# Additions moved to VectorE, unadded squares on TensorE, earlier weight splits, DMA-made tables and a later wait at the stage borders of a two-block transformer kernel

## What is computed

```python
def rms_norm(x, g):
    xf = x.astype(jnp.float32)
    y = xf * lax.rsqrt(jnp.mean(xf * xf, axis=-1, keepdims=True) + RMS_EPS)
    return (y * g.astype(jnp.float32)).astype(x.dtype)
...
        x = x + rms_norm(m, mix_post_g[layer])
        f = conv_glu_ffn(rms_norm(x, ffn_pre_g[layer]), ffn_w_in[layer], ffn_conv_w[layer],
                         ffn_conv_b[layer], ffn_w_out[layer])
        x = x + rms_norm(f, ffn_post_g[layer])
```

## Time and profile before

| | us |
|---|---|
| median of 3 runs (lowest to highest) | 1732.46 (1731.77 to 1732.62) |
| profiled execution, its own time | 1733.53 |
| its span in the trace | 1731.8 |
| PE busy | 1641.2 (95%) |
| DVE, ACT, POOL busy | 1028.8 (59%), 701.7 (41%), 286.4 (17%) |
| chain that ended last, on PE | 87% |

### The profile page before, as it was taken

The page is one execution under the profiler, slowest core; times in us unless marked ns, Lnnn a source line. Parts: engine busy times, 40 slices in busy tenths (PEclk is TensorE's granted clock), DMA queues, the critical chain, the costliest instruction groups (busy, mean ns, idle before and its releaser), DMA issues.

```text
span 1731.8 us, 21441 instructions
## 1 busy us (share of the span) xinstructions
PE 1641.2 (95%) x8098; PEld 1321.4 (76%) x8098; DVE 1028.8 (59%) x1860; ACT 701.7 (41%) x1370; POOL 286.4 (17%) x233
## 2 busy tenths in 40 slices
PE   6899999999898898999999998999998999999996
PEld 6678888888676686888888886866665788888875
DVE  4766666543768666666663266576666455554364
ACT  3444444332346644444442243243344243333252
POOL 2411111000402213111110025000001021110021
PEclk8899999999899999999999999999999999999998
DMA  4133333333121123333332324221110223333321
GB/s 142 37 97 96 96 97 97 104 97 92 52 70 34 38 61 86 97 98 97 97 96 95 96 63 110 67 55 38 43 39 24 86 82 96 97 97 98 98 91 61
DMA packets 89343, 139.28 MB, mean 80 GB/s; under 512 B 8596, under 2 KB 28564, under 8 KB 89240
## 3 DMA queue, kind: packets, MB, share of 16 engines
q1 hardware_dynamic: 86464, 133.56, 25.9%
q10 hardware_dynamic: 2776, 4.35, 0.9%
HBM read 135.78 MB, written 2.10 MB: 80 GB/s over the span
## 4 chain that ended last, share of the span: by engine, by line
PE 87%; DVE 6%; POOL 2%; issue 2%; ACT 1%; DMA 0%; SPq 0%; ACTq 0%; POOLq 0%; DVEq 0%
PE ps L399 23%; PE ps L401 22%; PE ps L400 22%; PE ps L1809 2%; PE ps L1811 2%; PE ps L1810 2%; POOL M L529 1%; PE ps L1492 1%; PE ps L1515 1%; PE ps L419 1%; PE ps L1535 1%; DVE Hl L514 1%; PE ps L412 1%; DVE M L681 1%; PE ps L456 1%
## 5 line engine op out<-in xcount | busy, mean ns | idle before, releaser
L387 DVE TENSOR_TENSOR wl<-raw,wh 128x512 fp32r<-128x512 f32 (+1 forms) x466 | 361.6, 779 | 481.0 <-ACT wh L376 480.9
L376 ACT ACTIVATE wh<-raw 128x512 fp32r<-128x512 f32 (+1 forms) x466 | 292.1, 628 | 648.6 <-PE ps L401 639.4
L399 PE MATMUL ps<-Hh,wh 128*128 128x512 f32 x1276 | 508.8, 399 | 17.6 <-DVE Hl L514 9.3
L400 PE MATMUL ps<-Hl,wh 128*128 128x512 f32 x1276 | 501.5, 393 | 0.0
L401 PE MATMUL ps<-Hh,wl 128*128 128x512 f32 x1276 | 501.3, 393 | 0.0
L399 PEld LDWEIGHTS ps<-Hh,wh 128*128 128x128 f32 x1276 | 242.6, 190 | 80.3 <-DVE Hl L514 14.9
L401 PEld LDWEIGHTS ps<-Hh,wl 128*128 128x128 f32 x1276 | 242.2, 190 | 52.0 <-issue 0.2
L400 PEld LDWEIGHTS ps<-Hl,wh 128*128 128x128 f32 x1276 | 242.6, 190 | 50.0 <-issue 0.9
L399 PE MATMUL ps<-AH,wh 128*128 128x512 f32 x456 | 177.6, 389 | 0.0
L401 PE MATMUL ps<-AH,wl 128*128 128x512 f32 x456 | 177.4, 389 | 0.0
L400 PE MATMUL ps<-AL,wh 128*128 128x512 f32 x456 | 177.4, 389 | 0.0
(11 more groups left out here) (291 smaller groups left out, 1925.3 us busy)
## 6 DMA issues: line engine op xcount, KB each, us to landing
raw<-in_w_in SPq DMA_DIRECT2D x216, 256.0 KB, 2.7
raw<-in_w_out SPq DMA_DIRECT2D x104, 256.0 KB, 2.6
raw<-in_w_up SPq DMA_DIRECT2D x64, 256.0 KB, 2.6
raw<-in_w_down SPq DMA_DIRECT2D x32, 256.0 KB, 2.7
raw<-in_w_q SPq DMA_DIRECT2D x16, 256.0 KB, 2.6
raw<-in_w_o SPq DMA_DIRECT2D x16, 256.0 KB, 2.6
raw<-in_w_pg SPq DMA_DIRECT2D x16, 256.0 KB, 2.8
X<-in_xT SPq DMA_DIRECT2D x8, 256.0 KB, 6.2
```

Source lines behind the costliest of these rows:

```text
L376: e.activation(split_in[n][0][:, 0:width], raws[n % NRAW][:, 0:width], ACT.Copy, scale=1.0 if gain is None else gain).then_inc(s_hi, 1)
L387: e.tensor_tensor(wl[:, 0:width], raw, wh[:, 0:width].bitcast(F32), ALU.subtract).then_inc(s_lo, 1)
L399: e.matmul(b, wh[:, o:o + w], xh, start=k == 0, stop=False, skip_group_check=joined)
L400: e.matmul(b, wh[:, o:o + w], xl, start=False, stop=False, skip_group_check=joined)
```

## The change

- `X_ON_POOL` is empty for the three borders with halves: all their additions of M to x are on DVE, and the order in `dve_new_rhs` is scale, low part of the column before, add.
- `rhs_sums` adds nothing there: PE takes the eight squares unadded, four calls of `mean_square` after piece 4 and four after piece 6.
- In the closing, DVE adds the squares of tiles 4 to 6 into `T[5]` (`add_square`), and PE sums `T[5]` and tile 7 alone, for each half; `first_four` is gone.
- Seven more pairs of buffers in each of the three borders instead of three. A table `due` lists what is split at each piece: from 14 pieces before `kv` and `z` and from 8 before `in1`, two pieces are split at a time, so that all eight pieces of the new group are split before the closing, and none is due at its pieces 0 to 4.
- `STAT_BANK` is the last bank instead of the last but one, and the wait for `RB` stands before the last of the four tiles of the next piece (`late`).
- The scaled tables come by DMA: `dist` grows from 256 KB to 2 MB, `cmp` from 62 to 496 KB. The DMA issues of ACT at the kv and z borders move from ahead of the border to piece 4 of the group.

The core of the diff:

```diff
--- before.py
+++ after.py
-for _n, _w in (("ident", 128), ("dist", 512), ("swa", 128), ("turn", 128), ("cmp", 124), ("sel", 512), ("band", 1088)):
+for _n, _w in (("ident", 128), ("dist", 4096), ("swa", 128), ("turn", 128), ("cmp", 992), ("sel", 512), ("band", 1088)):
...
-        more = [(sub(f"xh{i}", [P, NPIECE], 24576 + 4096 * i, F32R), sub(f"xl{i}", [P, NPIECE], 26624 + 4096 * i, F32R))
-                for i in range(3)]
+        more = [[(sub(f"xh{b}{i}", [P, NPIECE], o + 4096 * i, F32R), sub(f"xl{b}{i}", [P, NPIECE], o + 4096 * i + 2048,
+                  F32R)) for i in range(7)] for b, o in enumerate((0, 57856, 0))]
...
-            X_ON_DVE[v] = [(0, 0), (1, 0), (0, 1), (1, 1), (3, 1)]
-            X_ON_POOL[v] = [(2, 0), (2, 1), (4, 1), (5, 1), (6, 1), (7, 1)]
+            X_ON_DVE[v] = [(c, half) for half in range(2) for c in range(3)] + [(c, 1) for c in range(3, 8)]
+            X_ON_POOL[v] = []
...
+        AHEAD = ((first["kv"], first["out0"] + FT + 8), (first["in1"], first["o"] + 8),
+                 (first["z"], first["out1"] + FT + 8))
+
+        due, split_in, had_by, more_free = {}, {}, {}, {}
+        free_at = [(-1, None)] * (NSPL + 7)
+        n_due = 0
+        for n in range(-1, NP):
+            upto, border = n + 3, None
+            for b, (new, grow) in enumerate(AHEAD):
+                if grow <= n < new + 8:
+                    border = b
+                    upto = max(upto, min(n + 3 + min(n - grow + 1, 7), new + 7))
+            due[n] = list(range(n_due, min(upto, NP - 1) + 1))
+            n_due = max(n_due, upto + 1)
...
+        def high_ahead(e, n):
+
+            for m in due[n]:
+                split_high(e, m)
...
-        def multiply(e, n, outs, xh, xl, k, nk, closing=False, joined=False):
+        def multiply(e, n, outs, xh, xl, k, nk, closing=False, joined=False, late=None):
...
+                if late is not None and i == len(outs) - 1:
+                    e.wait_ge(*late)
...
-        STAT_BANK = 6
+        STAT_BANK = 7
...
         def rhs_sums(e, j):
-            i = 0
-            for c in range(KD):
+
+            i = 6 * (j > 3) + 6 * (j > 4)
+            for c in range(KD if j in (0, 4, 5) else 0):
...
-                if k == 6:
-                    e.wait_ge(s_sum, 6 * j + 3)
+                if k in (4, 6) and halved:
+                    for c in range(2 * k - 8, 2 * k - 4):
+                        e.wait_ge(s_sq, 8 * j + c + 1)
+                        mean_square(e, bank, M[:, c, :], c == 0, c == 7)
+                elif k == 6:
+                    i = 6 * (j > 3) + 6 * (j > 4)
+                    e.wait_ge(s_sum, i + 3)
                     mean_square(e, bank, M[:, 0, :], True, False)
-                    e.wait_ge(s_sum, 6 * j + 6)
+                    e.wait_ge(s_sum, i + 6)
                     mean_square(e, bank, M[:, 4, :], False, True)
...
-        def first_four(e, q):
-
-            e.wait_ge(s_merge, MERGES[q])
-            for half in range(2):
-                half_square(e, q, half, T[5], True, False)
...
-                        if k == 1 and half + i > 0:
-                            a, b = (half, i - 1) if i else (0, 3)
-                            e.wait_ge(s_psq, tile_at(q, 4 + b, a))
-                            half_square(e, q, a, T[POST_T[q][4 + b]], False, b == 3)
+                        if k == 1 and half and i == 0:
+                            e.wait_ge(s_qsum, 6 * q - 3)
+                            half_square(e, q, 0, T[5], True, False)
+                            e.wait_ge(s_psq, tile_at(q, 7, 0))
+                            half_square(e, q, 0, T[POST_T[q][7]], False, True)
                         if k == 1 and half and i == 3:
                             half_spread(e, q, 0)
+            e.wait_ge(s_qsum, 6 * q)
+            half_square(e, q, 1, T[5], True, False)
             e.wait_ge(s_psq, tile_at(q, 7, 1))
             half_square(e, q, 1, T[POST_T[q][7]], False, True)
...
+        def add_square(e, q, i, half):
+
+            n = 6 * (q - 1) + 3 * half + i
+            c = slice(256 * half, 256 * half + 256)
+            e.wait_ge(s_merge, MERGES[q])
+            e.wait_ge(s_psq, tile_at(q, 4 + i, half))
+            if n > 0:
+                e.wait_ge(s_qsum, n)
+            e.tensor_tensor(T[5][:, c], T[5][:, c], T[POST_T[q][4 + i]][:, c], ALU.add).then_inc(s_qsum, 1)
+
         def dve_close(e, q):
-            for i in range(4):
+            for i in range(3):
+                add_square(e, q, i, 0)
                 half_take(e, q, i, 0)
+            half_take(e, q, 3, 0)
             half_variance(e, q, 0)
-            half_take(e, q, 0, 1)
-            half_take(e, q, 1, 1)
+            for i in range(2):
+                half_take(e, q, i, 1)
+                add_square(e, q, i, 1)
             half_diagonal(e, q, 0)
+            add_square(e, q, 2, 1)
             half_take(e, q, 2, 1)
...
             elif q > 0:
-                if k < 4:
-                    scale_m(e, q, k + 4)
-                if k < 6:
+                if k < 5:
+                    scale_m(e, q, k + 3)
                     rhs_low(e, j, k + 2)
+                    add_m_dve(e, q, k + 3)
+                elif k == 5:
+                    rhs_low(e, j, 7)
...
-                    if k == 0 and g == 1:
-                        e.wait_ge(s_rb, j + 1)
-                    elif k == 0:
+                    if k == 0 and g > 1:
                         e.wait_ge(s_u, U0[l] + 4 * (g - 2) + 4)
-                    multiply(e, first[name] + 8 * g + k, outs, Hh[:, k, :], Hl[:, k, :], k, 8)
+                    multiply(e, first[name] + 8 * g + k, outs, Hh[:, k, :], Hl[:, k, :], k, 8,
+                             late=(s_rb, j + 1) if k == 0 and g == 1 else None)
...
-                add_m_pool(e, q)
+                    add_m_pool(e)
...
         def act_second(e):
-            e.wait_ge(*used[first["z"] - 1])
-            e.dma_start(dist[:, :], const("dist")).then_inc(s_dist, 16)
-            e.dma_start(cmpc[:, :], const("cmp")).then_inc(s_cmp, 16)
...
-                    split_high(e, MIX_PIECE[what] + k + 3)
+                    high_ahead(e, MIX_PIECE[what] + k)
+                    if what == "z0" and k == 4:
+                        e.wait_ge(*used[first["z"] - 1])
+                        e.dma_start(bias[:, :, :].rearrange("p h t -> p (h t)"), const("dist")).then_inc(s_dist, 16)
+                        e.dma_start(cb[:, :, :, :].rearrange("p b h n -> p (b h n)"), const("cmp")).then_inc(s_cmp, 16)
...
             half_root(e, 3, 0)
             half_root(e, 3, 1)
-            add_m_pool(e, 3)
             rhs_sums(e, 3)
-            e.wait_ge(s_dist, 16)
-            e.wait_ge(s_cmp, 16)
-            for h in range(8):
-                e.tensor_scalar(bias[:, h, :], dist[:, :], SLOPES[h], None, ALU.mult).then_inc(s_slope, 1)
-                e.tensor_scalar(cb[:, :, h, :], cmpc[:, :].rearrange("p (b n) -> p b n", b=4), SLOPES[h], None,
-                                ALU.mult).then_inc(s_slope, 1)
```

More of the change, by code:

```diff
@@ new lines, in build @@
+        due, split_in, had_by, more_free = {}, {}, {}, {}
[10 more added lines that the diff above has]
+            for m in due[n]:
+                places = range(NSPL)
+                if border is not None and m < AHEAD[border][0] + 8:
+                    dead = n - AHEAD[border][1] + 8 if border != 1 else 99
+                    places = [NSPL + i for i in range(7) if 2 * i + 1 < dead] + list(places)
+                at_ = next(i for i in places if free_at[i][0] <= n)
+                before = free_at[at_][1]
+                if at_ >= NSPL:
+                    split_in[m] = more[border][at_ - NSPL]
+                    if before is None or before < AHEAD[border][1]:
+                        more_free[m] = ((s_hl, rhs_at(3, 7)) if border == 1 else
+                                        used[AHEAD[border][1] - 8 + 2 * (at_ - NSPL) + 1])
+                        before = None
+                else:
+                    split_in[m] = spls[at_]
+                if before is not None:
+                    had_by[m] = before
+                held = [new for new, grow in AHEAD if new - 3 <= m < new]
+                free_at[at_] = (held[0] if held else m + 1, m)
@@ L686, in add_m_dve, with add_m_pool @@
             e.tensor_tensor(X[:, c, t], X[:, c, t], M[:, c, t], ALU.add).then_inc(s_xd, 1)
[L688 to L692 removed]
+        def add_m_pool(e):
+            for c, _ in X_ON_POOL[1]:
+                e.wait_ge(s_psc, scaled_at(0, c))
+                e.tensor_tensor(X[:, c, :], X[:, c, :], M[:, c, :], ALU.add).then_inc(s_xp, 1)
         def dve_new_rhs(e, q, j, k):
@@ L974, in pe_ffn @@
                     multiply(e, first[out] + nt * h + k, outs, AH[l][:, k, :], AL[l][:, k, :], k, nt, closing)
-                    if closing and k == 4:
-                        first_four(e, q + 1)
                 if closing:
@@ L1340, in act_window @@
                         act_rhs(e, 1, k)
```

(14 more changed lines are left out.)

103 lines of the change are left out of this document (40 added, 63 removed).

## The result

| | before | after |
|---|---|---|
| median of 4 runs each, us (lowest to highest) | 1732.54 (1731.77 to 1735.8) | 1716.3 (1715.36 to 1721.31) |
| profiled execution: own time, span | 1733.53, 1731.8 | 1717.08, 1715.3 |
| PE busy | 1641.2 (95%) | 1645.7 (96%) |
| POOL busy | 286.4 (17%) | 219.8 (13%) |

What follows compares the result with a forecast made beforehand. PE never rests in the long streams and pauses at stage borders. From 1733.5: -10.5 - 2.9 - 11.3 + 9.9 - 2.1 = -16.9, giving 1716.6, less 1.07: 1715.5 us; range 1704 to 1725.

Steps and rivals of the forecast that it cites:

- Closing: Closings at three borders: fewer one-column sums on PE, half additions covered on DVE; gain 10.5 us, between 5 and 12.
- rival B: Closing: DVE's chained additions come late, squares are awaited, half the gain goes; 1720.5 us, up to 1725; chance 0.2.
- DMA issues moved: kv and z borders: ACT's first Hh no longer waits for its own DMA issues; gain 2.9 us, range 1.5 to 4.
- First group: Piece 3 to next group, three borders: 21.35 us, waits gone through splits ahead and additions on DVE; net gain 11.3.
- rival D: DVE's 1.78 us splits come of the fp32r output, not POOL; five columns lose 1.5 us a border; 1720; chance 0.05.
- The clock: First groups: six runs of four one-column calls lower PE's clock, 1.65 us each; 9.9 us lost, range 0 to 15.
- Rival A: First groups: the clock stays up behind runs of four calls, the 9.9 us are not lost; 1705.6 us; chance 0.2.
- The rival of `two_a_piece`: First groups: clock follows how busy PE is, so falls stay with shorter runs of sums; 1716 us; no chance given.
- RB awaited late: in0, in2 and pp: a wait of some 0.7 us each goes; gain 2.1 us.
- z's gate: Gate matmul L1901 at z waits for what DVE takes with RB, so the 0.7 us gained there comes back.
- Rival C: Closings: doubled loads don't land in time, ACT's squares come late, PE waits; + 40 us, 1756; chance 0.05.
- Tables: Scaled tables by DMA, 2.5 MB instead of 0.3, and 16 POOL operations gone: both put at 0.

Runs made afterwards that it cites:

- after_again: The changed kernel itself, unaltered, run once more as base for the other runs of its chip: median 1715.48 us, ratio 0.9904.
- two_a_piece: Changed kernel with the eight one-column sums two at a time after pieces 3, 4, 5 and 6, not four after 4 and 6: 1703.68 us, ratio 0.9843.

## Why the prediction was right

- **Total:** 1715.5 against 1716.3 and 1715.48. That it is so near is luck as well. By the trace the closings gave 11.1 us (10.5 forecast), the way from the spread to piece 3 4.5 (3.5), RB 3.8 (2.1), and 1.1 came from an earlier start, which no term had. Against these stand losses that no term had either: 2.1 more at z's gate, 1.6 at 1182 us and 1.4 near the end.
- **Closing,** -10.5: 9.8 measured by undoing it, 11.1 by the trace. The half addition takes 0.43 us where 0.36 was estimated, and its cover held: PE has no idle time in the three closings, so none of rival B's waits is there.
- **DMA issues moved,** -2.9: 1.7 at z is confirmed, 0.4 at kv is 0, the 0.8 for the clock can't be told apart.
- **First group,** 21.35: 21.48 to 21.55. The size was right, the reason partly not. The prediction gave the gain to additions on DVE and to splits made ahead, since POOL stretches DVE's operations. The stretching is real (1.80 beside 0.68), which leaves nothing of rival D. But undoing both parts costs nothing in the median (1703.36), while giving POOL the squares back costs 4.2 us and brings back 2.7 to 3.0 of the wait of 3.96 us in the earlier trace rows. The other 1.0 of it must come of the additions that stood ahead of the sums on POOL; both together were not undone. The step that failed is "PE sets the pace. The 9 us for three pieces and the waits before piece 3 and piece 6 go", as far as it rests on a faster DVE: with DVE slow again the group takes 21.6 us instead of 21.5, and only the wait before piece 3 is back. Once PE reads the squares itself, its own sums stand between the pieces, and DVE may be late by a part of one.
- **The clock,** +9.9: 9.2 in the profile of the change, 12.2 in the second one, 11.8 by the medians, so 2.0 to 2.3 us a fall. Rival A is out: the clock falls within or behind four of the six runs of four calls in the profile of the changed kernel and all six in `after_again`, and nowhere in the group once the runs are of two. The rival of `two_a_piece`, by which the clock follows how busy PE is, is out too: the windows above have PE busy all 4.00 us, once at 0.95 and once at 0.50.
- **RB awaited late,** -2.1 at `in0`, `in2` and `pp`: undersized. From the two calls to the next group's first matmul it is 6.27 us before and 5.02 after, 1.25 a place and 3.8 in all, because I counted the idle time and not the distance of the starts. Inside the three groups the sum had 0.9 for the spread, and it is 0.46.
- **z's gate,** 0.7 given back: it was 1.25, and another 1.6 for the clock that fell behind the longer wait, which no term had.
- **Rival C:** its sign was there, its price was not. Ahead of the in1 closing, which starts at 612.75, ACT waits twice for a load before a split, 3.9 us in all; the trace of the kernel before has no such wait:

```profile
605.32 1.37 ACT L399 ACTIVATE xh<-raw 128x512 fp32r<-128x512 f32 x2 [2.78 <-DMA raw<-in_w_in]
607.83 0.63 ACT L399 ACTIVATE wh<-raw 128x512 fp32r<-128x512 f32 x1 [1.14 <-DMA raw<-in_w_in]
```

  The prediction named such a wait as a sign that it is wrong. But ACT had all eight pieces split by 614.7, and PE has no idle time between 594 us and the new x, so the doubled loads cost nothing there, by a small margin.
- **Tables:** 0, confirmed.

The terms add up along the trace. At the start of `in0`'s two calls the profile of the change is 1.1 us ahead (83.42 against 84.53), as it began sooner; `in0` gives 1.25, three `first_four` 2.9, the borders 14.4, the gate takes 1.25. That is 18.4, and the gate matmul comes 18.55 us sooner. Behind the gate 1.6 us go, and 1.6 more at 1182 us, where the clock fell behind a wait of 1.67 (0.66 from 1181 to 1185 us) that both kernels have and behind which it stayed up before (1.00 from 1198 to 1202). No part of the change lies there, and why it fell was not tried. `in2` and `pp` give 2.5. That is 17.9; the spans differ by 16.5, so 1.4 us are lost between `in2` and the end. Of these 0.8 come behind DVE's last operation, while the result is written out (4.31 us instead of 3.53). I have no cause for them.

## What to carry to other kernels

Read an engine's busy share together with the clock it was granted: here 21 us of idle time went, and some 9 to 12 came back as half-speed matmuls, because the work that filled the pause (one-column sums, four calls in a row) was followed by a clock of 0.50. Spreading the same sums in pairs between pieces kept it at 1.00 and made a version of 1703.68 us, 12 below the change and 27 below the kernel before; no other run is faster beyond the noise. When several parts lift the same wait, undo them one by one: the stretching that can be seen in the rows (1.78 us instead of 0.68) was not what the time hung on. And compare parts at an equal clock before calling one worthless: a gain of 1.2 us was hidden here by a clock that fell in some executions and not in others.

## What the runs showed of the hardware that was not expected

- A run of 32 recorded one-column matmuls (3.63 us at full clock) brought a granted clock near 0.50, within it or behind it, at 25 of 27 places in four traces; runs of 16 (1.84 us), four in a group with some 2.7 us of other matmuls between two, behind none of 84 in the seven traces that have them.
- How long it stays low differs between executions of the same instructions: 24.52 us or 26.10 for the same group at in1, with PEclk 0.86 or 0.79 over 24 us from its first run on.
- An SBUF addition on DVE that starts beside a POOL addition takes 1.80 us instead of 0.68; the low part of the same column, a moment later, keeps its 0.69, with POOL's sum over. In the kernel before, a low part beside POOL's sums takes 1.78.
- A wait of 2.1 us at the gate brought a fall behind it in ten of twelve traces, one of 1.04 and one of 1.15 did not; so 1 us more of idle time cost 2.6. At the new x waits of 0.91 to 0.98 us were followed by a fall at 14 of 32 borders.
- Behind the spread (L465) a ready matmul starts 0.46 us later; with a wait of 0.78 between them it is 1.80, so a wait can cost more than its idle time.
